# Two-layer hybrid encoder: the last down projection, the latents' norms and the final norm worked by halves of tokens

## The reference

```python
for layer in range(2):
    h = rmsnorm(x, attn_norm[layer])
    x = x + (even_mixer(h, ...) if layer == 0 else mla_mixer(h, ...))
    h = rmsnorm(x, ffn_norm[layer])
    x = x + (silu(h @ w_gate) * (h @ w_up)) @ w_down      # D_FF = 2816
return rmsnorm(x, final_norm)

def mla_mixer(h, w_in, q_norm, w_uq, kv_norm, w_uk, w_uv, w_out, t5_table):
    proj = h @ w_in                                   # 384 + 128 + 32 columns
    cq, ckv = rmsnorm(proj[:, :384], q_norm), rmsnorm(proj[:, 384:512], kv_norm)
    k_rope = rotate(proj[:, 512:], cos, sin)
    q, k_nope, v = cq @ w_uq, ckv @ w_uk, ckv @ w_uv  # 16 heads, dense attention
    ...
```

## Time and profile before

| | |
|---|---|
| median of 3 runs | 2888.35 us |
| profiled execution, its own time | 2887.91 us |
| its span | 2885.9 us |
| TensorE busy (PE) | 2714.1 us, 94% |
| VectorE busy (DVE) | 1735.6 us, 60% |
| POOL busy | 1423.1 us, 49% |
| ScalarE busy (ACT) | 955.8 us, 33% |
| mean granted clock of TensorE | 0.979 |

### The profile page before, as it was taken

How to read it: one execution, slowest core, us unless ns; L and a number is a source line. 1 busy time by engine, 2 the same in 40 slices (tenths; PEclk the granted TensorE clock), 3 DMA queues, 4 the chain that set the end, 5 groups by cost and what they waited for, 6 DMA issues and landing times. The chain is left out here.

```text
span 2885.9 us, 41180 instructions
## 1 busy us (share of the span) xinstructions
PE 2714.1 (94%) x13508; PEld 2251.5 (78%) x13508; DVE 1735.6 (60%) x2821; ACT 955.8 (33%) x1762; POOL 1423.1 (49%) x1332
## 2 busy tenths in 40 slices
PE   6899999989999999999884999999999999999996
PEld 4788888878788878878663888888887887878874
DVE  6565665564855555655545777777657555555555
ACT  3455544462411000111123666666623000111001
POOL 2333343466655556665511333333666555565554
PEclk9999999999999999999997999999999999999998
DMA  4433334344312111111214333433442111112112
GB/s 138 125 89 92 83 81 94 90 126 134 88 48 62 44 47 58 47 58 51 80 39 95 92 94 96 114 97 80 144 140 70 51 44 51 58 44 61 48 44 73
DMA packets 273161, 228.58 MB, mean 79 GB/s; under 512 B 44537, under 2 KB 237425, under 8 KB 272849
## 3 DMA queue, kind: packets, MB, share of 16 engines
q1 hardware_dynamic: 271079, 218.13, 27.6%
q10 hardware_dynamic: 1955, 8.83, 0.8%
...
## 5 line engine op out<-in xcount | busy, mean ns | idle before, releaser
L736 POOL TENSOR_SCALAR xT<-xT,rden 128x1024 f32<-128x1024 f32 (+2 forms) x256 | 280.7, 1096 | 685.4 <-DVE rden L1748 685.0
L777 POOL TENSOR_TENSOR ring<-block_t,ring 128x512 fp32r<-128x512 f32 x320 | 420.3, 1314 | 25.7
L775 POOL CAST ring<-block_t 128x512 fp32r<-128x512 f32 x320 | 214.5, 670 | 343.7 <-PE psD L1136 138.2
L1756 DVE TENSOR_TENSOR pt<-psD,pt 128x512 fp32r<-128x512 f32 (+2 forms) x512 | 303.5, 634 | 133.6 <-ACT pt L1347 133.1
L1102 PE MATMUL psS<-times_r,ring 128*128 128x512 f32 x928 | 365.8, 394 | 16.6 <-ACT rstd L1456 9.4
L1918 DVE TENSOR_TENSOR xT<-psD,xT 128x512 f32<-128x512 f32 x352 | 240.8, 690 | 205.1 <-PE psD L1136 205.1
L1104 PE MATMUL psS<-times_r,ring 128*128 128x512 f32 x928 | 362.2, 390 | 0.0
L1103 PE MATMUL psS<-times_r,ring 128*128 128x512 f32 x928 | 362.2, 390 | 0.0
L1347 ACT ACTIVATE pt<-psD 128x512 fp32r<-128x512 f32 (+2 forms) x512 | 258.0, 557 | 150.1 <-PE psD L937 149.1
L1134 PE MATMUL psD<-act,ring 128*128 128x512 f32 x704 | 281.3, 400 | 12.8 <-DVE act L1890 6.7
L1336 ACT ACTIVATE xT<-xT,mneg 128x1024 f32<-128x1024 f32 (+2 forms) x256 | 273.4, 1068 | 48.1 <-DVE mneg L1740 48.1
...
## 6 DMA issues: line engine op xcount, KB each, us to landing
...
kq<-split_x SPq DMA_DIRECT2D x130, 128.0 KB, 2.4
kq<-row SPq DMA_DIRECT2D x126, 128.0 KB, 2.3
...
heads<-o_out SPq DMA_DIRECT2D x128, 64.0 KB, 2.1
```

What stands on the lines that cost most here:

```text
L736: pool.tensor_scalar(s, s, rden[:, t % 4:t % 4 + 1], 1.0, ALU.mult, ALU.mult).then_inc(S["normed"], 1)
L777: pool.tensor_tensor(lo, src, hi.bitcast(F32), ALU.subtract).then_inc(S["ws"], 1)
L1756: ve.tensor_tensor(PT[:, 1, j0:j1, t % 3, :], blocks(psT[b][:, 0:(j1 - j0) * P]), PT[:, 0, j0:j1, t % 3, :].bitcast(F32), ALU.subtract).th ...
```

## The change

The order of halves is h=1 first, then h=0, from the last down projection to the norm. `last_down` takes five banks; its weights are split into the place of an operand that the last turn has read. For `norm_a1`, ScalarE and VectorE split x * gain at once, without the root, and the root of the norm is multiplied in when a half column of latents is read out (`latent_out`). Squares, sums, means and roots are made by halves. Latents are multiplied in ten groups (column, half) in the order of `GROUPS_C`, with the means of the latents between groups; their weights are loaded into the blocks of the MLP and split in the order of `SPLIT_C`. Key rotation is by halves. `park` is issued by SP after the last sum, and the sine rows for the rotation are loaded when it has landed. The first pair's products run in the order 0, 1, 2, 4, 6, 7 before the loop, 3 and 5 behind the first tile; SP copies head 0's operands first. The table for the second mixer is built one addition a step (9 and 11, 5 and 7), and SP's load of offsets moves from step 5 to 7. The final norm is by halves, h=1 first, its first root under the last products. The diff, cut; an addition here stands for the matching removal of the code above.

```diff
+GROUPS_C = ((3, 1), (3, 0), (4, 0), (0, 0), (1, 0), (2, 0), (0, 1), (1, 1), (4, 1), (2, 1))
+SPLIT_C = (3, 2, 1, 4, 0)
 ORDER_C = (2, 0, 3, 1, 4, 5, 6, 7)
...
+last_banks = [quarters[n] for n in ("S0a", "S0b", "S1a", "D2", "D3")]
+latent_banks = [quarters[n] for n in ("S1b", "D0", "S0a", "S0b", "S1a", "D0", "S1b", "S0b", "S0a", "S1a")]
...
+        if t0 == 0:
+            sp.wait_ge(S["b_tab"], 2 * QB)
+        early_x(ph, src, 0, (7, 3))
     if step == 11:
         column_weights(ph, w, 2)
...
-sp.wait_ge(S["nl"], at("norm_a1", "nl", 16))
-sp.wait_ge(S["ws"], at("attn_c", "ws", -1))
+for n, c in enumerate(SPLIT_C):
+    blocks_free = (("ffn_0", 33, NFF - 2), ("ffn_0", 18, NFF - 1), ("ffn_0", 20, NFF - 1), ("latent", 2, 0),
+                   ("latent", 1, 0))[n]
+    sp.wait_ge(S["ws"], at(blocks_free[0], "ws", blocks_free[1], blocks_free[2], UNITS))
+    b, width = (0, 2, 4, 2, 0)[n], P if c < 4 else ROPE
+    sp.dma_start(block_t[:, b:b + 2, :].rearrange("p b c -> p (b c)")[:, 0:KT * width]
+                 .rearrange("p (k c) -> p k c", k=KT),
+                 w_odd[:, c * P:c * P + width].rearrange("(k p) c -> p k c", p=P)).then_inc(S[f"lw{c}"], 16)
+sp.wait_ge(S["xa"], at("ffn_0", "xa", 16, NFF - 1, 16))
+sp.dma_start(park[:, :], xT[:, :]).then_inc(S["pk"], 16)
+sp.wait_ge(S["ms"], at("norm_a1", "ms", 2))
 for j in range(4):
     rows, src = slice(j * ROPE, (j + 1) * ROPE), (cos, sin)[j % 2]
     sp.dma_start(cos_t[rows, :], src[rows, :]).then_inc(S["cs"], 16)
-sp.dma_start(xT[0:ROPE, SIN:SIN + SEQ], sin[0:ROPE, :]).then_inc(S["cs"], 16)
 uq = w_uq.rearrange("(k p) (h c) -> k p h c", p=P, c=UQ)
 def latent_weights(pair):
...
 latent_weights(0)
-sp.wait_ge(S["kr_lo"], at("latent", "kr_lo", 1))
-for h in range(3):
+sp.wait_ge(S["pk"], at("norm_a1", "pk", 1))
+sp.wait_ge(S["nl"], at("norm_a1", "nl", 16))
+sp.dma_start(xT[0:ROPE, SIN:SIN + SEQ], sin[0:ROPE, :]).then_inc(S["cs"], 16)
+rel_table(rel_c, TILES, 0, 0)
+latent_weights(1)
+for n in (0, 1):
+    move_c(0, n, 0)
+sp.wait_ge(S["kr_lo"], at("latent", "kr_lo", 2))
+for o, b in zip(latent_ops(0)[2:], latent_ops(0)[2:]):
+    sp.dma_start(o[UQ:P, :].bitcast(F32), b[HD:UQ, :].bitcast(F32)).then_inc(S["kr0"], 16)
+for n in (2, 4):
+    move_c(0, n, 0)
+sp.wait_ge(S["lt"], at("latent", "lt", 10))
+for n in (0, 1, 2, 4):
+    move_c(0, n, 1)
+for h in range(1, 3):
     for a, b in zip(latent_ops(h)[2:], latent_ops(0)[2:]):
-        for o in (HD, UQ) if h else (UQ,):
+        for o in (HD, UQ):
             sp.dma_start(a[o:o + ROPE, :].bitcast(F32), b[HD:UQ, :].bitcast(F32)).then_inc(S["kr_in"], 16)
-rel_table(rel_c, TILES, 0, 0)
+for n in (3, 5):
+    for e in range(2):
...
-    pool.wait_ge(S["whi"], at(ph, "whi", n + 1, it, per))
-    pool.tensor_tensor(lo, src, hi.bitcast(F32), ALU.subtract).then_inc(S["ws"], 1)
 def half_split(ph, n, half, hi, lo, b):
@@ -808,15 +835,47 @@
         split_down(ph, it, 23, (4, 4), [("pu", 21, 14), ("pu", 22, 14), ("pu", 23, 14), ("dn", 4, 16)])
         split_matrix(ph, "up", it, 27, 1, (5, 5), [("dn", 8, 16), ("dn", 12, 16), ("dn", 16, 16)]
                      + [("pu", 24 + k, 14) for k in range(4)])
-    split_down(ph, NFF - 1, 16, (4, 3), [("pu", 14, 14), ("pu", 15, 14), ("pu", 16, 14), ("dn", 4, 16)])
-def add_squares(ph):
+    pool.wait_ge(S["pu"], at(ph, "pu", 24, NFF - 2, 14))
+    for d in range(4):
+        n = BLOCKS["down"][d]
+        pool.wait_ge(S[f"sb{n}"], at(ph, f"sb{n}", (4, 3)[d // 2], NFF - 1, 2))
+        pool.tensor_copy(last_unit(d, 0), block_t[:, n, :]).then_inc(S["whi"], 1)
+        pool.wait_ge(S["whi"], at(ph, "whi", 17 + d, NFF - 1, UNITS))
+        pool.tensor_tensor(last_unit(d, 1), block_t[:, n, :], last_unit(d, 0).bitcast(F32), ALU.subtract)\
+            .then_inc(S["ws"], 1)
...
+def add_squares(ph, part):
+    h = 1 - part
     for j in range(1, KT - 1):
-        pool.wait_ge(S["sq"], at(ph, "sq", j + 1))
+        pool.wait_ge(S["sq"], at(ph, "sq", KT * part + j + 1))
         if j > 1:
-            pool.wait_ge(S["sqm"], at(ph, "sqm", j - 1))
-        pool.tensor_tensor(rstd[:, :], rstd[:, :], sq_t[:, j % 2, :], ALU.add).then_inc(S["sqm"], 1)
+            pool.wait_ge(S["sqm"], at(ph, "sqm", 6 * part + j - 1))
+        pool.tensor_tensor(square_place(h, 0), square_place(h, 0), square_place(h, j), ALU.add)\
+            .then_inc(S["sqm"], 1)
+def column_of_latents(n):
+    c = SPLIT_C[n]
+    b, cols = (0, 2, 4, 2, 0)[n], KT * (P if c < 4 else ROPE)
+    src = block_t[:, b:b + 2, :].rearrange("p b c -> p (b c)")[:, 0:cols]
+    pool.wait_ge(S[f"lw{c}"], at("latent", f"lw{c}", 1))
+    if c == 4:
...
+        pool.wait_ge(S["pu"], at("ffn_0", "pu", 30, NFF - 2, 14))
+    pool.tensor_copy(latent_w(c, 0), src).then_inc(S["whi"], 1)
+    pool.wait_ge(S["whi"], at("latent", "whi", n + 1))
...
 proj_weights("proj_0", 0)
 ffn_weights("ffn_0")
-add_squares("norm_a1")
-pool.wait_ge(S["pu"], at("latent", "pu", 0))
-for n in range(5):
-    split("latent", n, n % 3, ("sc", n - 2, 0) if n >= 3 else None,
-          cols=KT * P if n < 4 else KT * ROPE)
-pool.wait_ge(S["sc"], at("attn_c", "sc", 0))
+for n in range(2):
+    column_of_latents(n)
+add_squares("norm_a1", 0)
+column_of_latents(2)
+add_squares("norm_a1", 1)
+for n in range(3, 5):
+    column_of_latents(n)
 for half in range(2):
     latent_split(0, half)
+for h in range(2):
+    add_latents(h)
+pool.wait_ge(S["lt"], at("latent", "lt", 10))
...
+def mean_of_part(ph, part, to):
+    h = 1 - part
+    if part:
+        pe.wait_ge(S["sr"], at(ph, "sr", 1))
+    pe.wait_ge(S["sqm"], at(ph, "sqm", 6 * (part + 1)))
+    pe.wait_ge(S["sq"], at(ph, "sq", KT * (part + 1)))
+    pe.matmul(to, ones[:, :], square_place(h, 0), start=True, stop=False)
+    pe.matmul(to, ones[:, :], square_place(h, KT - 1), start=False, stop=True).then_inc(S["ms"], 1)
...
+def last_down(ph, norm=None):
+    pe.wait_ge(S["sl"], at(ph, "sl", 8, NFF - 2, 4))
+    pe.wait_ge(S["xa"], at(ph, "xa", 0, NFF - 1, 16))
+    for n in range(2 * KT):
+        h, m = 1 - n // KT, n % KT
+        if m == 0:
+            pe.wait_ge(S["al"], at(ph, "al", 3 if h else 4, NFF - 1, 4))
+        if n < KT and m % 2 == 0:
+            pe.wait_ge(S["ws"], at(ph, "ws", 17 + m // 2, NFF - 1, UNITS))
+        if n >= 5:
+            pe.wait_ge(S["xa"], at(ph, "xa", n - 4, NFF - 1, 16))
+        o, c = last_banks[n % 5], slice(h * HALF, (h + 1) * HALF)
+        for f in range(2):
+            w = slice(f * 2 * P + m % 2 * P, f * 2 * P + (m % 2 + 1) * P)
+            hi, lo = last_unit(m // 2, 0)[:, w], last_unit(m // 2, 1)[:, w]
+            pe.matmul(o, hi, act[:, f, 0, c], start=f == 0, stop=False)
+            pe.matmul(o, hi, act[:, f, 1, c], start=False, stop=False)
+            mm = pe.matmul(o, lo, act[:, f, 0, c], start=False, stop=f == 1)
+        mm.then_inc(S["dn"], 1)
+        if norm and n == 10:
+            mean_of_part(norm, 0, psD[1])
 proj("proj_0", 0, "norm_f0")
 ffn("ffn_0", "norm_f0")
-pe.wait_ge(S["xa"], at("norm_a1", "xa", 0))
...
-    for c in range(2):
-        if h == 0:
-            pe.wait_ge(S["ws"], at("latent", "ws", c + 1))
-        mm = product(psS[c], h, range(KT), lambda s, k, c=c: whalf(c, s, k), h_of,
...
+def latent_group(g):
+    c, h = GROUPS_C[g]
+    if GROUPS_C[:g].count((c, 1 - h)) == 0:
+        pe.wait_ge(S["ws"], at("latent", "ws", SPLIT_C.index(c) + 1))
+    if g == 2:
+        pe.wait_ge(S["xa"], at("ffn_0", "xa", 16, NFF - 1, 16))
+    elif g == 8:
+        pe.wait_ge(S["kr_lo"], at("latent", "kr_lo", 1))
+    elif g > 4:
+        pe.wait_ge(S["raw"], at("latent", "raw", {5: 2, 6: 1, 7: 4, 9: 5}[g]))
+    width = P if c < 4 else ROPE
+    o = latent_banks[g][0:width, :]
+    for k in range(KT):
+        if g < 2:
+            pe.wait_ge(S["nl"], at("norm_a1", "nl", KT * g + k + 1))
+        w = slice(k * width, (k + 1) * width)
+        pe.matmul(o, latent_w(c, 0)[:, w], h_of(0, k, h), start=k == 0, stop=False)
+        pe.matmul(o, latent_w(c, 0)[:, w], h_of(1, k, h), start=False, stop=False)
+        mm = pe.matmul(o, latent_w(c, 1)[:, w], h_of(0, k, h), start=False, stop=k == KT - 1)
+    mm.then_inc(S["lt"], 1)
...
+def mean_of_latents(n, to):
+    if n < 2:
+        pe.wait_ge(S["sq"], at("latent", "sq", n + 1))
+    else:
+        pe.wait_ge(S["sqm"], at("latent", "sqm", 2 * (n - 1)))
+    if n >= 2:
+        pe.wait_ge(S["nl"], at("latent", "nl", 2 + 3 * (n - 2)))
+    pe.matmul(to, ones[:, :], latent_squares[min(n, 2)], start=True, stop=True).then_inc(S["ms"], 1)
+latent_group(0)
+mean_of_part("norm_a1", 0, psD[1])
+latent_group(1)
+mean_of_part("norm_a1", 1, psD[3])
+latent_group(2)
+mean_of_latents(0, psD[1])
+latent_group(3)
+mean_of_latents(1, psD[3])
+for g in range(4, 7):
+    latent_group(g)
+mean_of_latents(2, psD[1])
+for g in range(7, 10):
+    latent_group(g)
 def c_product(pair, n):
...
 def c_operands(h):
     qh, ql, kh, kl = latent_ops(h)
     return [(qh, kh), (qh, kl), (ql, kh)]
-for n in ORDER_C:
+for n in (0, 1):
+    c_product(0, n)
```

(102 more changed lines are left out.)

419 lines of the change are left out of this document (212 added, 207 removed).

## The result

The changed kernel takes 2823.72 us (median of 4 runs, 2821.92 to 2825.09), the kernel before 2888.61 in the same session (2886.62 to 2889.50): a ratio of 0.9771, 95% interval 0.9759 to 0.9783, 64.9 us less. The forecast was 2825. The profiled spans are 2821.0 and 2885.9 us.

What follows compares the result with a forecast made beforehand. TensorE, busy 94% of the span, was taken to bound the kernel, losing time only where idle or at low clock. Gains of 53 + 6.4 + 4 = 63.4 us gave 2825 us; own case 2817 to 2834, wider range 2808 to 2850.

Steps and rivals of the forecast that it cites:

- Part 1: Last down projection by halves: starts 0.9 us earlier, its 96 products still take 24.8 us, 15 at half clock.
- stall taken 0: Last down projection: TensorE not held up by VectorE's slower groups beside POOL; 0 us, bounds 0 and 8.
- Part 2: First latents without their root: TensorE goes on after the down projection, removing the 11.2 us hole and slow 25.6 us.
- Part 3: Latents' norm: sine rows wait for the store of x, TensorE stalls 4.6 us; first bias 59.6 us earlier, 53 after deductions.
- Part 4: Even attention's second-mixer tables moved to steps with filler products: three waits of 2.15 us go, 6.4 us; the fourth gives 0.
- 3.5 for hops: Chain to the odd attention's first bias: 3.5 us taken off the gain for some 30 hops counted at almost nothing.
- What moved into the loop: First tiles of the odd attention's loop: 18 products, two evictions and one rotary lo moved there cost 3 us.
- Part 5: Final norm by halves: one reciprocal and eight scalings halfway under the chain to the second root; 4 us, bounds 1 and 6.
- A: Rival, 20%: VectorE's chain through the latents bounds, not TensorE; 2840 us.
- B: Rival, 12%: the stall at the latents' norm doesn't come, as the store lands early and hops are as counted; 2812 us.
- C: Rival, 3%: slower, the joined stretch of 384 products stays at half clock; 2893 us.
- D: Rival, 1.5%: it does little, the gain being given back inside the attention, whose first tiles something else bounds.

Runs made afterwards that it cites:

- the one-column run: Changed kernel with GpSimd adding one column of each square instead of 512 in the norms behind both last down projections: 2818.98 us, ratio 0.9758 to the kernel before.
- the sine run: Changed kernel with the sine rows loaded early into separate SBUF and the store of x issued after the first latent weights and cosines: 2818.33 us against 2822.78.
- final norm late: Changed kernel with the final norm's first half (mean, root, reciprocal, eight scalings) after the last product and last sum: 2822.79 us, ratio 0.9767 to the kernel before.
- roots first: Changed kernel with both means, roots and reciprocals made before the first latent group: 2836.81 us, ratio 0.9814 to the kernel before.
- operands late: Changed kernel with the operands of the first latent products made after the last down projection instead of under it: 2826.94 us, ratio 0.9786 to the kernel before.

## Why the prediction was right

*Part 1.* The start came 0.9 us earlier, as forecast: TensorE's wait ahead of it is 2.51 us, before 3.39, and it is released by the third low part (0.68 us at 1399.12). The first line is the kernel before:

```profile
1408.31 0.80 PE L1134 MATMUL psD<-act,ring 128*128 128x512 f32 x1 [3.39 <-DVE act L1890]
```
```profile
1400.06 0.47 PE L1203 MATMUL psS<-act,times_r 128*128 128x512 f32 x1 [2.51 <-DVE act L2036]
```

The piece of the table hides it (668.8 for 668.6), because the loop ahead took 1.2 us longer in this trace; among the twelve traces in which that code is the same the piece runs from 667.7 to 669.7. What was wrong is the clock: 15 products at half clock in the forecast, none in the profiled run, and the down projection takes 22.8 us instead of 24.8. VectorE's groups took 1.7 us beside GpSimd's additions and 2.8 where GpSimd split a column, 1.84 on average, not 1.9, and TensorE waited only for twice 0.2 us; the last sum ended 30.5 us after the start, forecast 32.4 (1439.8 less 1407.4). But "stall taken 0" missed what the one-column run shows: this pace sets the store, and 5.9 us of S with it. The forecast had the two links (pace, store behind the last sum) and priced them apart. VectorE's last low part ends 10.5 us behind TensorE's last product; the forecast named some 8, and its own times give 9.0.

*Part 2.* No hole up to 1468, as forecast. Its two overlaps are worth 12.4 to 13.0 us (roots) and 4.5 to 5.1 us (operands) at the first bias, 10.6 and 2.5 us in S, each measured with the rest kept; the larger part of S's 54.5, the latents and their norm by halves with the second mixer's read-outs inside them, was not undone by itself and is read only from the stretches.

*Part 3.* The step held: the wait for the sine behind the store (5.8 us), TensorE's wait at the mean ahead of group 7 (3.7, forecast 4.6), the last mean (1.4, forecast 1.5), and the sine run removes the first two for 4.6 us. First bias 59.5 us earlier apart from part 4, forecast 59.6 less 3.5 for hops. From the start to the first bias it takes 106.0 us, forecast 107.1 and 3.5 for hops. The store was issued 2.0 us earlier than forecast (30.5 us after the start for 32.5), the rotation followed it in 18.7 us instead of 17.6, and from there to the first bias it took 56.8 us, forecast 57.0 without a hop: the 3.5 us for hops weren't needed. (The forecast's terms for the sine rows add up to 1457.1, not 1457.5.)

*What moved into the loop* was sized right, but the clock there was not foreseen: 5.3 us up to the ninth bias (33.1 from the first, before 27.8 by the earlier trace rows's instruction), forecast 3. The 18 products are in one block ahead of the third tile's scores. In the changed kernel the clock falls within TensorE's wait of 3.8 us for the copies and is low (half) from 1500.7 to 1510.9: the scores ahead of the block and its first five products run at half clock, the block takes 5.3 us, and the second bias waits until 6.7 us after the first because VectorE's eviction, ahead of it, waits for the block. In three traces with the same code there (final norm late, roots first, operands late) the clock is back before the block: it takes 4.2 to 4.3 us, the second bias comes 4.5 us after the first, the ninth 30.9 to 31.0. That is 3.1 us more than before, the forecast's 3; the other 2.2 are the clock. The stretch from the first bias to the second (columns as in the first fence), in the changed kernel and with the final norm late:

```profile
1506.10:1512.80 6.70, 6.64 (x19) 5.32 (x20) 1.91 (x6) 1.88 (x3) 0.00 (x0) 0.64 0.83 180
```
```profile
1507.50:1512.00 4.50, 4.37 (x19) 3.68 (x20) 1.93 (x6) 1.93 (x3) 0.00 (x0) 1.00 0.94 207
```

*Part 4.* 6.6 of 6.4, by four waits shortened, not three removed.

*Part 5.* 2.4 us, forecast 3.1 behind the start and 0.9 at it. Of the latter TensorE's wait shows 0.6 (2.8 us, before 3.3), though the piece that holds it came out 0.3 us longer. The times held: first root 24.1 us after the start (forecast 25.1), second 35.3 (34.8), end of the last scaling 44.9 (44.1). The reason didn't. "What was hidden by nothing is halfway under the chain to the second root" isn't where the gain is, since without the overlap the tail is the same: VectorE's two reciprocals and 16 scalings, 17.4 us, follow the first root in every order tried. The sign named for this part, the last output half 4 us closer to the last down product, came in part: it is 3.1 us closer (22.6 us behind that product's end, before 25.8).

*Rivals.* A (20%) didn't come: in the query groups VectorE has spare time (it stands idle 5.7 us ahead of the third reciprocal of the latents), and the sine run turns its whole gain into time. B (no stall at all) didn't either: the wait at the mean was 3.7 us. Nor did C, as the joined stretch has a granted clock of 1.00 for 68 us, nor D, as the attention kept all but 5.3 us of the earlier first bias.

The sum is right to 1.5 us (63.4 forecast, 64.9 measured) partly by errors that cancel, by the pieces of the table: +2.1 and -1.1 before the down projection, +2.4 in S, -1.2 and -0.7 behind it. Within S the hops (+3.5) and the earlier store less its longer way (+0.9) outweigh the half clock at the loop's start (-2.2). The down projection's clock isn't a term of its own in this sum: it acts only through VectorE's last sum and so is part of the earlier store. That the total is within 1.3 us of the measured time is therefore in part luck.
